# A Fourier and retention trunk on one core: homes for the start slots, an earlier split of h, gates ahead of rstd

## The chip, the core and the metric

The kernel runs on one core of a Trainium2 chip. The metric is the time of one execution on the device in microseconds (us). The engines are named as in the profile: PE (TensorE; PEld is its weight load), DVE (VectorE), ACT (ScalarE), POOL (GpSimd), SP (SyncE, which here only issues DMAs).

## The reference

Two layers work on 512 latent and 256 context tokens of width 1024. Each layer norms its input and modulates it by rows that come from the condition vectors `c` and `c_ctx` (`ada_params`). Layer 0 mixes by a grouped 2-D Fourier transform, layer 1 by bidirectional retention with four heads. Both gate with `silu(z)` and project back.

```
def ada_params(cond, w, b):
    m = jax.nn.silu(cond) @ w + b
    return jnp.split(m, 3, axis=-1)
def fourier_mixer(h, w_in, w_out):
    u, z = jnp.split(h @ w_in, 2, axis=-1)
    y = jnp.fft.fft2(ug, axes=(1, 3), norm='ortho').real     # ug: u in 8 groups of 256
    return (y * jax.nn.silu(z)) @ w_out
def ret_output(o, z, w_out):
    o = o * lax.rsqrt(jnp.mean(o * o, axis=-1, keepdims=True) + EPS)
    return (o * jax.nn.silu(z)) @ w_out
    ...
    hl = rmsnorm(x, norm_g[i]) * (1.0 + sc_l[:, None, :]) + sh_l[:, None, :]
    x = x + gt_l[:, None, :] * ol
```

## The kernel before, in words

**Weights.** All weights come in one stream of 512 KB slots, `stream[t]`, issued by SP in order. A slot lands in one of three buffers of `raw`, is split by ACT into a rounded part (`hi`) and by DVE into the rest (`lo`), both into `ring`, and PE multiplies with three matmuls per product (`mm3`). SP waits before each load until the buffer's last user is done.

**Start.** Slots 0 to 15 hold the adaptive norm's weights of layer 0 and aren't split. The string `START` says who consumes slot t: `P` is PE (`ada_tile`, 16 matmul records on the raw tile), `D` is DVE (`early`, two dot products with the condition rows `cond_rows`). Slots 0 to 7, all for PE, give the scale; all eight must be done before DVE can make the factor `fmul`. Beside them the six token tiles `x_tok` arrive. ACT squares them (`x_root`), DVE inverts the roots (`x_rstd`), folds tile pairs (`x_fold`) and splits them with ACT (`x_hi`, `x_lo`). Then PE runs the token transform `transform(k)` for k = 0 to 7, with an `ada_tile` of slots 9, 11, 13 and 15 behind k = 0 to 3. After each transform ACT and DVE write its two parts (`transform_lo`), and DVE runs `early` of slots 8, 10, 12 and 14 between them. Slots 8 to 15 give the shift (`add_shift`), which the second half of U group 0 needs. A load of slot t waits for the user of slot t - 3.

**U groups.** `project_u(g)` for eight groups, then `features`. Meanwhile POOL makes h (`tmp_t`). After group 7, ACT and DVE split the slots z0 and z1, the U result (`u_hi`, `u_lo`), and copy and combine the features (`copy_q`, `sum_diff`); then they split h in eight parts (L791, L1258). PE's next work, `gates(0, 0)`, waits for all of group 7's split (`u_lo_done`) and for part k of h at its step k. It writes the context halves to bank 2, which group 7 has used.

**Last head.** After the last head, PE starts the output projection `out_pair(SLOT_OUT1, ...)`. At step 3 it sums the squares (`o_sum`, L1856). ACT takes the root, DVE the reciprocal (L1390). DVE then multiplies the four head outputs with it into `p_f` (L1408), and `p_f` is multiplied into the gates, two of them by POOL (L643) and two by DVE (L1412). Only then does DVE split slot 2 of the output weights (L1038), which PE needs for step 8. The queue order on each engine is that of the code.

Of the kernel before, what the change touches and what calls it, by code (L numbers as in the profile page):

```python
# [66 lines left out]
START = "PPPPPPPPDPDPDPDP"  # L67
DVE_SHIFT = 4
# [13 lines left out]
    "u": (SLOT_U, 3, 1, (6, 5, 5)),  # L82
    "z": (SLOT_Z, 3, 2, (11, 11, 10)),
    "out0": (SLOT_OUT0, 2, 0, (27, 27, 26)),
    "head": (SLOT_HEAD, 3, 2, (35, 35, 26)),
    "out1": (SLOT_OUT1, 2, 0, (51, 51, 42)),
# [71 lines left out]
def build(nc, x_lat, x_ctx, x_rows, small_in, cond_in, decay_in, stream, tables_in, middle_in,  # L158
          middle_w_in, rope_in, out):
    ctx = ExitStack()  # L160
    with ctx:
# [72 lines left out]
        squares = gate[:, 11 * D:12 * D].bitcast(mybir.dt.bfloat16).rearrange("p (b n) -> p b n", b=2)  # L234
# [44 lines left out]
        fold = xreg[:, 4128:4128 + 2 * SLOT].rearrange("p (b n) -> p b n", b=2)  # L279
        q_f = gate[:, TT * D + P + 2 * TOK:TT * D + P + 2 * TOK + NF]  # L280
# [43 lines left out]
        s_raw = [sem(f"raw_in{i}") for i in range(RAW_BUFS)]  # L324
        s_xt, s_rope, s_out = sem("x_columns_in"), sem("rope_in"), sem("out_stored")
# [58 lines left out]
        def _(sp):  # L384
# [16 lines left out]
            def load_start(t):  # L401

                if t >= RAW_BUFS:
                    used(t - RAW_BUFS)
                buf = raw_at("start", t)[0]
                sp.dma_start(raw[:, buf, :], stream[t]).then_inc(s_raw[buf], 16)

            def load_x(t):
                sp.dma_start(x_tok[:, t, :], x_rows[t]).then_inc(s_x[t], 16)

            load_x(0)
            load_x(1)
            load_start(0)
            load_x(2)
            load_x(3)
            load_start(1)
            load_x(4)
            load_x(5)
            load_start(2)
# [40 lines left out]
        def _(pool):  # L460
# [178 lines left out]
            def gate_head(h, tiles=range(4)):  # L639
                for i in tiles:  # L640
# [22 lines left out]
            gate_head(HEADS - 1, (0, 2))  # L663
# [10 lines left out]
        def _(act):  # L674
# [22 lines left out]
            def x_root(t):  # L697
                act.wait_ge(s_x[t], 16)
                if t >= 2:
                    act.wait_ge(tok_sq, t - 1)  # L700
# [322 lines left out]
        def _(dve):  # L1023
# [165 lines left out]
            for k in range(KT):  # L1189
                transform_lo(k)  # L1190
                if k < DVE_SHIFT - 1:
                    early(KT + 2 * k + 2)
# [921 lines left out]
```

## Time and profile before

| | us |
|---|---|
| median of 3 runs | 985.59 (983.39 to 987.88) |
| the profiled execution | 989.9 |
| its span, first to last instruction | 988.1 |
| PE busy / DVE busy / ACT busy / POOL busy in it | 941.5 / 547.6 / 345.0 / 258.7 |

Times inside the execution are counted from the start of the span. The mean granted clock of PE was 0.977 of full speed; a stretch at 0.50 is at the lower of its two levels (1.2 of 2.4 GHz).

### The profile page before, as it was taken

What the parts mean: (1) busy time and instruction counts of PE and PEld (TensorE: products, weight loads), DVE (VectorE), ACT (ScalarE), POOL (GpSimd) and SP (SyncE); (2) the same over time, 40 slices, a digit from 0 to 9 for tenths busy, and PEclk for the clock granted to TensorE, in tenths of its full rate; (3) what the DMA queues carried; (4) which work ended last, traced back from release to release, by engine and by line L of the source; (5) the groups of instructions that cost most, each with busy time, mean ns of one, the idle gap of its engine ahead of it and who ended that gap; (6) DMA issues with size and microseconds to landing.
All of it is one profiled execution on the core that took longest, in us unless ns stands there. A gap on an engine that the chain in (4) does not pass through costs nothing.

```text
span 988.1 us, 13089 instructions
## 1 busy us (share of the span) xinstructions
PE 941.5 (95%) x4838; PEld 811.9 (82%) x4838; DVE 547.6 (55%) x810; ACT 345.0 (35%) x582; POOL 258.7 (26%) x251
## 2 busy tenths in 40 slices
PE   5899998999999999959999999999999999998996
PEld 5798998888888888847888888887888888876886
DVE  4666876999985332358344355426434445456433
ACT  6342434333314332334333333324223333453222
POOL 3338970477764000014100131014100321011001
PEclk9899999999999999979999999999999999998998
DMA  7645332565555211211222021102211121102222
GB/s 300 221 157 181 121 110 86 180 193 183 192 172 229 68 64 64 85 42 48 81 64 65 22 86 64 65 22 69 80 64 42 42 69 58 64 1 81 90 86 86
DMA packets 28858, 98.70 MB, mean 100 GB/s; under 512 B 3816, under 2 KB 6024, under 8 KB 28560
## 3 DMA queue, kind: packets, MB, share of 16 engines
q1 hardware_dynamic: 26384, 89.86, 27.1%
q0 software_dynamic: 2032, 7.89, 2.2%
q8 instruction: 26, 0.43, 0.2%
q10 hardware_dynamic: 400, 0.39, 0.1%
q14 instruction: 16, 0.13, 0.0%
HBM read 96.01 MB, written 2.10 MB: 99 GB/s over the span
## 4 chain that ended last, share of the span: by engine, by line
PE 85%; DVE 6%; DMA 3%; POOL 2%; issue 2%; ACT 1%; SPq 0%; POOLq 0%; DVEq 0%; ACTq 0%
PE banks L1618 27%; PE banks L1619 27%; PE banks L1620 27%; DMA raw<-stream 3%; PE banks L1671 2%; DVE hreg L1373 1%; POOL gate L643 1%; DVE xreg L1432 1%; DVE gate L1367 1%; DVE ring L1038 1%; DVE gate L1397 0%; POOL gate L636 0%; POOL xreg L653 0%; PE banks L1856 0%; POOL gate L670 0%
## 5 line engine op out<-in xcount | busy, mean ns | idle before, releaser
L1618 PE MATMUL banks<-hreg,ring 128*128 128x512 f32 (+2 forms) x940 | 336.4, 358 | 19.9 <-DVE hreg L1373 9.1
L1619 PE MATMUL banks<-hreg,ring 128*128 128x512 f32 (+2 forms) x940 | 333.8, 355 | 0.0
L1620 PE MATMUL banks<-hreg,ring 128*128 128x512 f32 (+2 forms) x940 | 331.3, 352 | 0.0
L1038 DVE TENSOR_TENSOR ring<-raw,ring 128x512 fp32r<-128x512 f32 x192 | 134.8, 717 | 272.9 <-ACT ring L682 272.2
L682 ACT ACTIVATE ring<-raw 128x512 fp32r<-128x512 f32 x192 | 119.5, 630 | 387.7 <-PE banks L1620 313.2
L1618 PEld LDWEIGHTS banks<-hreg,ring 128*128 128x128 f32 x940 | 178.8, 190 | 48.3 <-issue 12.9
L1620 PEld LDWEIGHTS banks<-hreg,ring 128*128 128x128 f32 x940 | 178.4, 190 | 22.9
L1619 PEld LDWEIGHTS banks<-hreg,ring 128*128 128x128 f32 x940 | 178.9, 190 | 22.0 <-issue 1.0
L603 POOL TENSOR_TENSOR gate<-xreg,gate 128x257 f32<-128x257 f32 (+1 forms) x64 | 81.5, 1304 | 68.6 <-ACT gate L817 51.3
L1070 DVE CUSTOM_DVE_ANT_0 dist<-raw,gate 128x1024 bf16<-128x1024 f32 x64 | 90.5, 1414 | 3.8
L636 POOL TENSOR_TENSOR gate<-gate 128x512 f32<-128x512 f32 x12 | 16.8, 1397 | 250.7 <-ACT gate L891 249.9
L1618 PE MATMUL banks<-ring,hreg 128*128 128x512 f32 x192 | 74.7, 389 | 0.0
L1619 PE MATMUL banks<-ring,hreg 128*128 128x512 f32 x192 | 74.7, 389 | 0.0
L1620 PE MATMUL banks<-ring,hreg 128*128 128x512 f32 x192 | 74.7, 389 | 0.0
L1618 PE MATMUL banks<-wreg 128*128 128x512 f32 (+2 forms) x192 | 71.8, 374 | 0.0
L1619 PE MATMUL banks<-wreg 128*128 128x512 f32 (+2 forms) x192 | 71.2, 371 | 0.0
L1620 PE MATMUL banks<-wreg 128*128 128x512 f32 (+2 forms) x192 | 71.1, 370 | 0.0
L1619 PE MATMUL banks<-wreg,ring 128*128 128x512 f32 (+2 forms) x172 | 58.8, 342 | 0.0
L1620 PE MATMUL banks<-wreg,ring 128*128 128x512 f32 (+2 forms) x172 | 58.4, 339 | 0.0
L1618 PE MATMUL banks<-wreg,ring 128*128 128x512 f32 (+2 forms) x172 | 58.3, 339 | 0.0
L1671 PE MATMUL banks<-csf,raw 128*128 128x128 f32 x192 | 30.4, 328 | 16.6 <-DMA raw<-stream 16.6
L651 POOL TENSOR_TENSOR xreg<-xreg 128x512 f32<-128x512 f32 x8 | 10.4, 1295 | 126.1 <-DVE xreg L1432 126.1
(214 smaller groups left out, 1142.2 us busy)
## 6 DMA issues: line engine op xcount, KB each, us to landing
raw<-stream SPq DMA_DIRECT2D x160, 512.0 KB, 3.3
gate<-x_rows SPq DMA_DIRECT2D x6, 512.0 KB, 6.8
gate<-x_lat POOLq DMA_DIRECT2D x1, 2048.0 KB, 8.8
xreg<-x_lat POOLq DMA_DIRECT2D x1, 2048.0 KB, 9.2
gate<-cond_in POOLq DMA_DIRECT2D x2, 512.0 KB, 7.2
gate<-x_ctx POOLq DMA_DIRECT2D x1, 1024.0 KB, 11.5
xreg<-x_ctx POOLq DMA_DIRECT2D x1, 1024.0 KB, 12.0
xreg<-tables_in SPq DMA_DIRECT2D x1, 775.0 KB, 11.5
```

Of the source, the lines that this page charges most:

```text
L603: pool.tensor_tensor(g, y, g, ALU.mult).then_inc(gated, 1)
L636: pool.tensor_tensor(head_rstd, head_rstd, p_f[:, i % 2, :], ALU.add).then_inc(oacc, 1)
L643: pool.tensor_tensor(g, g, p_f[:, i % 2, :], ALU.mult).then_inc(ogated, 1)
L651: pool.tensor_tensor(turn[0], turn[0], turn[1], ALU.subtract).then_inc(summed, 1)
L682: act.activation(ring[:, n % 2, 0, c], raw[:, buf, c], ACT.Copy).then_inc(hi_done, 1)
L1038: dve.tensor_tensor(ring[:, n % 2, 1, c], raw[:, buf, c], f32(ring[:, n % 2, 0, c]), ALU.subtract).then_inc(split_done, 1)
L1070: dve.tensor_tensor_reduce(out=dot_out, in0=raw[:, buf, :], in1=cond_rows[:, v, :], scale=1.0, scalar=0.0, op0=ALU.mult, op1=ALU.add, accu ...
L1367: dve.tensor_tensor(tmp_t[:, k, 0:LAT], tmp_t[:, k, 0:LAT], rstd_t[:, 0:LAT], ALU.mult).then_inc(t_vec, 1)
L1618: pe.matmul(out, left[0], right[0], start=start, stop=False)
L1619: pe.matmul(out, left[0], right[1], start=False, stop=False)
L1620: return pe.matmul(out, left[1], right[0], start=False, stop=stop)
L1671: last = pe.matmul(o, raw[:, buf, P * k:P * k + P], csf[:, k:2 * KT:KT].unsqueeze(1).to_broadcast([P, WARM, 2]), start=k == 0, stop=k == K ...
```

## The change

It has three independent parts.

1. **Start.** Slots 3 to 8 get places of their own (`ada_home`: the two `fold` buffers, a free piece of `gate`, and token tiles 0, 2 and 1 once those are used up), so that with the three `raw` buffers nine slots have one each. The condition rows are loaded by SP behind slot 5, no longer by POOL. The small decay load goes behind slot 8. Slot 15 is consumed by DVE in place of PE (`START` ends in `DD`, `DVE_SHIFT` is 5). ACT loads the root table ahead of the first token tile, and squares token tile 5 before it waits for the reciprocal of tile 4, which DVE makes earlier. The first `add_shift` and `fold_lo(0)` both stand after transform 5.
2. **End of the U groups.** ACT and DVE split parts 0 and 1 of h ahead of the second half of z1 and of group 7's result, part 2 ahead of `copy_q(6)` and `sum_diff(6)`. PE no longer waits for group 7's split before `gates(0, 0)`, whose context halves go to bank 7.
3. **Last head.** DVE multiplies the four outputs into their gates before the reciprocal (`last_products`). Behind the reciprocal DVE splits slot 2 first, then DVE and POOL multiply two gates each with the reciprocal in place.

```
-START = "PPPPPPPPDPDPDPDP"
-DVE_SHIFT = 4
+START = "PPPPPPPPDPDPDPDD"
+DVE_SHIFT = 5
...
+        ada_home = [fold[:, 0, :], fold[:, 1, :], gate[:, 11 * D:12 * D], x_tok[:, 0, :],
+                    x_tok[:, 2, :], x_tok[:, 1, :]]
+        def ada_slot(t):
+            if RAW_BUFS <= t <= KT:
+                return ada_home[t - RAW_BUFS], s_ada[t - RAW_BUFS], 16
+            buf, landed = raw_at("start", t if t < RAW_BUFS else t - len(ada_home))
+            return raw[:, buf, :], s_raw[buf], landed
...
             def load_start(t):
-                if t >= RAW_BUFS:
-                    used(t - RAW_BUFS)
+                if t in (6, 7):
+                    sp.wait_ge(pair_done, 2 * (t - 5))
+                if t == KT:
+                    sp.wait_ge(xs_lo, 2)
+                if t > KT:
+                    used(t - RAW_BUFS if t > KT + RAW_BUFS else t - KT - 1)
...
+            for t in range(3, 6):
+                load_start(t)
+            for v in range(2):
+                sp.dma_start(cond_rows[:, v, :], cond_in[v].partition_broadcast(P)).then_inc(s_cond, 16)
+            for t in (6, 9, 7, 10, 8):
+                load_start(t)
             sp.dma_start(dk[:, 0, :], decay_in.partition_broadcast(P)).then_inc(s_decay, 16)
-            for t in range(RAW_BUFS, SLOT_U):
+            for t in range(11, SLOT_U):
                 load_start(t)
...
-            pool.wait_ge(s_x[TT - 1], 16)
-            for v in range(2):
-                pool.dma_start(cond_rows[:, v, :], cond_in[v].partition_broadcast(P)).then_inc(s_cond, 16)
...
-            gate_head(HEADS - 1, (0, 2))
+            pool.wait_ge(orstd, HEADS)
+            for i in (0, 2):
+                pool.wait_ge(onorm, 4 * (HEADS - 1) + i + 1)
+                g = gate1[:, FT - 4 + i, :]
+                pool.tensor_tensor(g, g, head_rstd, ALU.mult).then_inc(ogated, 1)
...
             act.activation(csf[:, :], small[:, 0:16], ACT.Silu).then_inc(csf_done, 1)
+            act.activation(small[:, 0:1], eps[:, :], ACT.Sqrt).then_inc(warm, 1)
...
             x_root(4)
+            x_root(5)
             act.wait_ge(tok_rstd_done, 5)
...
-            x_root(5)
...
-            u_hi(GROUPS - 1)
-            copy_q(GROUPS - 2)
             act.wait_ge(slot_done, 2 * SLOT_Z + DONE0)
             for k in range(KT):
                 act.wait_ge(h_made, 2 * k + 2)
                 act.activation(h_hi[:, k, :], tmp_t[:, k, :], ACT.Copy).then_inc(hhi_done, 1)
+                if k == 1:
+                    hi("z", 1, SLOT_Z + 1, halves=(1,))
+                    u_hi(GROUPS - 1)
+                if k == 2:
+                    copy_q(GROUPS - 2)
...
+            def last_products():
+                dve.wait_ge(z1_done, 4 * HEADS)
+                for i in range(4):
+                    dve.wait_ge(osq, 4 * (HEADS - 1) + i + 1)
+                    g = gate1[:, FT - 4 + i, :]
+                    dve.tensor_tensor(g, bank(2 + i), g, ALU.mult).then_inc(onorm, 1)
...
+            last_products()
             for kk in range(8, 12):
                 g1_lo(kk)
             o_rstd(HEADS - 1)
+            lo("out1", 2, RING_OUT1 + 2)
             last_norm()
-            lo("out1", 2, RING_OUT1 + 2)
...
-                lat, ctx_out = (3 * q, 3 * q + 1), 3 * q + 2
+                lat, ctx_out = (3 * q, 3 * q + 1), 7 if first else 3 * q + 2
...
-            pe.wait_ge(u_lo_done, 2 * GROUPS)
             gates(0, 0, first=True)
```

SP's queue at the start, before (a load of a start slot reads `raw<-stream`; behind the third one, the tables, the decay row, then slots 3 to 15):

```order
L406 DMA raw<-stream 128x1024
L420 DMA xreg<-tables_in 128x1550
L422 DMA dk<-decay_in 128x8
L406 DMA raw<-stream 128x1024 [waits ada_slot_used] x8
L406 DMA raw<-stream 128x1024 [waits early_dot_done]
L406 DMA raw<-stream 128x1024 [waits ada_slot_used]
```

And of the change (slots 3, 4 and 5, the condition rows, then slots 6, 9, 7, 10, 8, the decay row, 11 and 12, 13):

```order
L429 DMA xreg<-tables_in 128x1550
L420 DMA xreg<-stream 128x1024 x2
L420 DMA gate<-stream 128x1024
L434 DMA gate<-cond_in 128x1024 x2
L420 DMA gate<-stream 128x1024 [waits x_folded]
L420 DMA raw<-stream 128x1024 [waits ada_slot_used]
L420 DMA gate<-stream 128x1024 [waits x_folded]
L420 DMA raw<-stream 128x1024 [waits ada_slot_used]
L420 DMA gate<-stream 128x1024 [waits x_lo_done]
L437 DMA dk<-decay_in 128x8
L420 DMA raw<-stream 128x1024 [waits ada_slot_used] x2
L420 DMA raw<-stream 128x1024 [waits early_dot_done]
```

Five transfers between the tables and slot 6 no longer wait for anything, and the waits of slots 6, 7 and 8 are on the folding and splitting of the tokens and no longer on PE's tiles.

DVE at the end of the U groups, before (`ring` are the halves of z0 and z1, `wreg` is group 7's split, `xreg` is `sum_diff(6)`, `hreg` the parts of h):

```order
L1038 TENSOR_TENSOR ring<-raw,ring 128x512 x4
L1215 TENSOR_TENSOR wreg<-banks,wreg 128x386 x2
L1225 TENSOR_TENSOR xreg<-banks,gate 128x386 x2
L1258 TENSOR_TENSOR hreg<-gate,hreg 128x768 x8
```

And of the change:

```order
L1056 TENSOR_TENSOR ring<-raw,ring 128x512 x3
L1274 TENSOR_TENSOR hreg<-gate,hreg 128x768 x2
L1056 TENSOR_TENSOR ring<-raw,ring 128x512
L1234 TENSOR_TENSOR wreg<-banks,wreg 128x386 x2
L1274 TENSOR_TENSOR hreg<-gate,hreg 128x768
L1244 TENSOR_TENSOR xreg<-banks,gate 128x386 x2
L1274 TENSOR_TENSOR hreg<-gate,hreg 128x768 x5
```

Two parts of h now stand ahead of five other instructions; nothing is added.

DVE behind the last head, before (`hreg` are the splits of gates 6 to 11, then the reciprocal, norms and gates, slots 2 and 3, the splits of gates 12 to 15):

```order
L1417 TENSOR_TENSOR hreg<-gate,hreg 128x512 x6
L1390 RECIPROCAL gate<-gate 128x512
L1408 TENSOR_TENSOR gate<-banks,gate 128x512 x2
L1412 TENSOR_TENSOR gate<-gate 128x512
L1408 TENSOR_TENSOR gate<-banks,gate 128x512 x2
L1412 TENSOR_TENSOR gate<-gate 128x512
L1038 TENSOR_TENSOR ring<-raw,ring 128x512 x4
```

And of the change:

```order
L1427 TENSOR_TENSOR gate<-banks,gate 128x512 x4
L1439 TENSOR_TENSOR hreg<-gate,hreg 128x512 x4
L1411 RECIPROCAL gate<-gate 128x512
L1056 TENSOR_TENSOR ring<-raw,ring 128x512 x2
L1435 TENSOR_TENSOR gate<-gate 128x512 x2
L1056 TENSOR_TENSOR ring<-raw,ring 128x512 x2
L1439 TENSOR_TENSOR wreg<-gate,wreg 128x512 x4
```

Nothing stands between the reciprocal and the split of slot 2 any more; the four multiplications that stood there are ahead of the reciprocal.

## Rows read from the trace of the kernel before

**Rows 1.** The page, part 4: the chain that ended last, by engine.

```profile
PE 85%; DVE 6%; DMA 3%; POOL 2%; issue 2%; ACT 1%; SPq 0%; POOLq 0%; DVEq 0%; ACTq 0%
```

**Rows 2.** Windows, an undisturbed stretch: A:B length, busy, clock, DMA share, GB/s.

```profile
75.00:155.00 80.00, 80.00 (x451) 77.22 (x450) 55.00 (x85) 29.22 (x55) 63.47 (x57) 1.00 0.37 129
```

**Rows 3.** The page, part 6: issues, KB each, median us to landing.

```profile
raw<-stream SPq DMA_DIRECT2D x160, 512.0 KB, 3.3
...
gate<-cond_in POOLq DMA_DIRECT2D x2, 512.0 KB, 7.2
```

**Rows 4.** The chain in order of time, start: start us, us, what.

```profile
19.84 5.48 PE banks L1671 x32
...
25.34 7.25 DMA raw<-stream
...
32.63 3.79 PE banks L1671 x16
...
44.50 5.76 DMA raw<-stream
...
56.44 1.83 PE banks L1671 x16
...
60.80 0.17 PE banks L1618
```

**Rows 5.** Timelines of PE, POOL, ACT, DVE, start: start us, us, instruction [idle before].

```profile
7.87 6.89 PE L1671 MATMUL banks<-csf,raw 128*128 128x128 f32 x32 [7.87 <-DMA raw<-stream]
15.26 2.06 PE L1671 MATMUL banks<-csf,raw 128*128 128x128 f32 x16 [0.49 <-DMA raw<-stream]
...
39.51 2.00 PE L1671 MATMUL banks<-csf,raw 128*128 128x128 f32 x16
...
50.31 2.64 PE L1671 MATMUL banks<-csf,raw 128*128 128x128 f32 x16 [1.92 <-DMA raw<-stream]
...
17.24 2.85 POOL L523 CAST wreg<-xreg 128x516 fp32r<-128x516 f32 x2 [14.71 <-DMA xreg<-tables_in]
...
6.42 1.28 ACT L704 ACT_TABLE_LOAD   x1
...
19.51 1.15 ACT L723 ACTIVATE gate<-gate,dist 128x1024 f32<-128x1024 f32 x1 [3.10 <-DVE dist L1105]
...
29.21 1.22 DVE L1127 TENSOR_TENSOR ring<-gate,ring 128x1024 fp32r<-128x1024 f32 x1
...
65.64 1.28 DVE L1056 TENSOR_TENSOR ring<-xreg,ring 128x512 fp32r<-128x512 f32 x2
```

**Rows 6.** Windows, while the condition rows are in flight.

```profile
26.00:28.00 2.00, 2.00 (x20) 2.00 (x20) 2.00 (x2) 1.98 (x2) 0.00 (x0) 1.00 0.82 152
```

**Rows 7.** Timelines of ACT, DVE and PE at the U groups' end.

```profile
153.44 0.63 ACT L682 ACTIVATE ring<-raw 128x512 fp32r<-128x512 f32 x1 [1.44 <-PE banks L1620]
...
155.59 5.98 ACT L791 ACTIVATE hreg<-gate 128x768 fp32r<-128x768 f32 x8
...
156.67 7.03 DVE L1258 TENSOR_TENSOR hreg<-gate,hreg 128x768 fp32r<-128x768 f32 x8
...
157.76 0.77 PE L1618 MATMUL banks<-hreg,ring 128*128 128x512 f32 x1 [2.60 <-DVE hreg L1258]
```

**Rows 8.** Windows, PE behind three of its waits (the clock stands before the DMA share).

```profile
157.76:162.00 4.24, 4.24 (x15) 3.62 (x16) 4.24 (x6) 3.81 (x6) 0.00 (x0) 0.64 0.02 4
896.67:902.00 5.33, 5.33 (x14) 4.19 (x15) 4.17 (x7) 0.02 (x1) 0.00 (x0) 0.54 0.61 185
50.31:56.44 6.13, 6.13 (x40) 6.13 (x41) 2.88 (x6) 0.00 (x0) 0.14 (x1) 0.72 0.70 215
```

**Rows 9.** The chain behind the last head.

```profile
887.55 3.36 DVE gate L1390
...
896.02 0.61 DVE ring L1038
```

**Rows 10.** Timeline of PE behind the last head.

```profile
896.67 0.80 PE L1618 MATMUL banks<-hreg,ring 128*128 128x512 f32 x1 [4.42 <-DVE ring L1038]
```

More of the change, by code:

```diff
@@ L81 @@
     "start": (0, 3, 0, (0, 0, 0)),
[L82 to L86, printed above, removed]
+    "u": (SLOT_U, 3, 1, (4, 3, 3)),
+    "z": (SLOT_Z, 3, 2, (9, 9, 8)),
+    "out0": (SLOT_OUT0, 2, 0, (25, 25, 24)),
+    "head": (SLOT_HEAD, 3, 2, (33, 33, 24)),
+    "out1": (SLOT_OUT1, 2, 0, (49, 49, 40)),
 }
@@ L324, in build @@
         s_raw = [sem(f"raw_in{i}") for i in range(RAW_BUFS)]
+        s_ada = [sem(f"ada_in{i}") for i in range(RAW_BUFS, KT + 1)]
         s_xt, s_rope, s_out = sem("x_columns_in"), sem("rope_in"), sem("out_stored")
@@ L637, in norm_head, with gate_head @@
                                        ALU.add).then_inc(oacc, 1)
-            def gate_head(h, tiles=range(4)):
-                for i in tiles:
+            def gate_head(h):
+                for i in range(4):
                     pool.wait_ge(onorm, 4 * h + i + 1)
@@ L674, in _, with hi @@
         def _(act):
-            def hi(phase, n, r, i=0, per=0):
+            def hi(phase, n, r, i=0, per=0, halves=(0, 1)):
                 buf, landed = raw_at(phase, n)
                 act.wait_ge(s_raw[buf], raw_step(phase, per) * i + landed if per else landed)
-                for a in range(2):
+                for a in halves:
                     c = slice(a * SLOT // 2, (a + 1) * SLOT // 2)
@@ L698, in x_root @@
                 act.wait_ge(s_x[t], 16)
-                if t >= 2:
-                    act.wait_ge(tok_sq, t - 1)
-                act.activation(squares[:, t % 2, :], x_tok[:, t, :], ACT.Square,
+                act.activation(squares, x_tok[:, t, :], ACT.Square,
                                accum_out=tok_ss[:, t:t + 1]).then_inc(tok_sq, 1)
@@ L814, in gates @@
                     for a, b, src in ((0, LAT, bank(3 * q + half)),
-                                      (LAT, TOK, bank(3 * q + 2, CTX, CTX * half))):
+                                      (LAT, TOK, bank(7 if first else 3 * q + 2, CTX, CTX * half))):
                         kk = 2 * j + half if split is not None else gate0_at(2 * j + half)
@@ L1030, in link, with lo @@
                 dve.wait_ge(step, steps[0])
-            def lo(phase, n, r):
+            def lo(phase, n, r, halves=(0, 1)):
                 buf = raw_at(phase, n)[0]
-                for a in range(2):
+                for a in halves:
                     c = slice(a * SLOT // 2, (a + 1) * SLOT // 2)
@@ L1130, in early @@
             def early(t):
-                buf, landed = raw_at("start", t)
+                src, s_landed, landed = ada_slot(t)
                 d = START[:t].count("D")
-                dve.wait_ge(s_raw[buf], landed)
+                dve.wait_ge(s_landed, landed)
                 dve.wait_ge(cond_rows_done, 2)
@@ L1191, in _ @@
                 if k < DVE_SHIFT - 1:
-                    early(KT + 2 * k + 2)
-                if k == 4:
+                    early((10, 12, 14, 15)[k])
+                if k == 5:
                     dve.wait_ge(early_dot, 2 * DVE_SHIFT)
@@ L1259, in _ @@
                                   ALU.subtract).then_inc(hlo_done, 1)
+                if k == 1:
+                    lo("z", 1, SLOT_Z + 1, halves=(1,))
+                    u_lo(GROUPS - 1)
+                if k == 2:
+                    sum_diff(GROUPS - 2)
             def gates(jj, q, split=None, first=False, last=False):
@@ L1666, in ada_tile @@
             def ada_tile(t, o):
-                buf, landed = raw_at("start", t)
-                pe.wait_ge(s_raw[buf], landed)
+                src, s_landed, landed = ada_slot(t)
+                pe.wait_ge(s_landed, landed)
                 for k in range(KT):
-                    last = pe.matmul(o, raw[:, buf, P * k:P * k + P],
+                    last = pe.matmul(o, src[:, P * k:P * k + P],
                                      csf[:, k:2 * KT:KT].unsqueeze(1).to_broadcast([P, WARM, 2]),
```

59 lines of the change are left out of this document (24 added, 35 removed).

## The prediction

> **What bounds the kernel now.** I read the page first, then the chain in order of time, then the timelines and windows around the chain's steps that aren't PE. PE carries 85% of the chain [rows 1], and between 75 and 155 us it is busy for all of 80.00 us at clock 1.00 [rows 2]: there nothing is to be won without taking work from PE. The reader should look for the places where PE stands still, and for the clock behind them. There are three groups.
>
> At the start the chain goes from load to tile and back: tiles 3 and 4, the load of slot 7 that was issued at 25.34 once tile 4 had given its buffer back and took 7.25 us, tile 7 from 32.63 to 36.42, and later the load of slot 13, 5.76 us from 44.50 [rows 4], for which PE stood still for 1.92 us [rows 5]. At the end of the U groups PE waits 2.60 us for the first part of h [rows 7]. Behind the last head it waits 4.42 us [rows 10] for slot 2, which DVE splits only after the reciprocal, the norms and the gates [rows 9].
>
> Each wait is paid twice. Behind them PE ran at a mean clock of 0.64 for 4.24 us, 0.54 for 5.33 us, and 0.72 for 6.13 us [rows 8], with the lower level in them. What a stretch lost is its length times what its clock lacks of 1: 1.53, 2.45 and 1.72 us.
>
> **Part 1, the start.** The question is when slot 7 lands. From slot 0 (tile 0 starts at 7.87) to slot 2 (15.26) six 512 KB transfers landed [rows 5], so one took 7.39 / 6 = 1.23 us, or 426 GB/s, with the queue full. The tables landed at 17.24 [rows 5]. But slot 3, which is behind the decay row, let tile 3 start only at 19.84 [rows 4], 2.6 us later in place of 1.23. In the change the decay row is behind slot 8, and slots 3, 4, 5, two condition rows, 6, 9 and 7 follow the tables, none with a wait that isn't over by then (the last one, on the fold of tiles 2 and 3, is over before the second split of tokens starts). Eight transfers by 1.23 put slot 7 at 27.1. The condition rows may cost more: while they were in flight, 152 GB/s moved at a busy share of 0.82 [rows 6], 185 GB/s for full engines. At that rate their 1.05 MB take 5.7 us and not 2.5, and slot 7 lands at 30.3. Those are the two bounds; slot 7's other traffic speaks for neither, and I take the middle, 28.7.
>
> PE has tiles 3 to 7 to run from 18.5. At full clock one takes 1.83 us, and tiles 3 and 4, partly at the lower level, took 5.48 together [rows 4]; 18.5 + 5.48 + 3 x 1.83 = 29.5 even so. So the load still decides: tile 7 ends at 28.7 + 1.83 = 30.5, against 36.42: **5.9 us**. Tokens are no bound: their last split ended at 30.43 [rows 5], is wanted only by the last operands of the first transform, and the change takes up to 1.28 (the table load ahead of the first tile) and 3.10 us (ACT's wait for a reciprocal) [rows 5] out of that chain. These two edits I cost at nothing more; without them the tokens would end about when they are wanted.
>
> The first transform then runs without half clock: it took 39.51 - 36.42 = 3.1 us [rows 4, 5], a later one 60.80 - 58.27 = 2.5 [rows 4]: **0.6 us**. Slot 15's tile leaves PE: **1.8 us** [rows 4]. DVE takes its two dots, and with them the first shift and the fold's split (1.28 us [rows 5]) move together behind transform 5. I estimate that `transform_lo(6)` is 1 us late and PE starts U group 0 that much later. This costs next to nothing, since its second half waits for the shift of parts 4 to 7 anyhow; should the pile reach that shift, it costs at most the 1.28.
>
> What becomes of the wait for slot 13? Its load is let go by DVE's dots of slot 10, behind the first `transform_lo`, and the transforms run to where it is wanted at the same distance as before. Slots 12 and 14 are in flight beside it as before, so I take the same 5.76 us, and the 1.92 + 1.72 = 3.6 us stay. The page's median is 3.3 us [rows 3]; with that, slot 13 would be there in time. The Trainium skill, "DMA: Bandwidth & Descriptors", section "Anatomy of one DMA", gives a fixed 2.0 us and the bytes at 436 GB/s, 3.2 us for 512 KB by my estimate; the median agrees, this load does not. By that rule the sum for the start would be 3.6 us larger.
>
> Start: 5.9 + 0.6 + 1.8 = 8.3 us. Bounds: slot 7 at 30.3 and tile 7 at half clock (3.79 us [rows 4]) end at 34.1, 3.6 later, and the 0.6 goes too: 4.1. Tile 7 at 29.5 and slot 13 in time: 8.3 + 1.0 + 3.6 = 12.9.
>
> **Part 2, the U groups' end.** ACT is let go by PE's last U matmul at 153.44; one part of h costs it 5.98 / 8 = 0.75, and DVE 7.03 / 8 = 0.88 us [rows 7]. So part 0 is split at 155.1, and PE is free at 157.76 - 2.60 = 155.2. The wait goes, with the loss of clock behind it: 2.60 + 1.53 = **4.1 us**. What is late next is group 7's split, the second half of z1 and `sum_diff(6)`. PE wants them at its step 4 and behind it, and one step ahead of them (six matmuls on 512 and six on 256 columns) costs it more than the 0.88 of a part of h. Parts 1 to 3 keep ahead. Bank 7 costs nothing, as its last reader was group 0. The lower bound is 2.3, a few tenths of wait and the clock lost all the same.
>
> **Part 3, the last head.** The reciprocal ends at 887.55 + 3.36 = 890.91 [rows 9]. The first half of slot 2 then costs 0.61 [rows 9] and is there at 891.5; PE reaches step 8 at 896.67 - 4.42 = 892.25 [rows 10]. The wait goes and so does the loss behind it: 4.42 + 2.45 = **6.8 us**. The four products come ahead, while POOL still adds squares and DVE waits, so the reciprocal needn't be later. It has 0.7 us to give. Behind slot 2 the gates now take one pass each, on two engines, and the second slot and gates 12 to 15 are wanted four steps later. The lower bound is 4.0.
>
> Sum: 8.3 + 4.1 + 6.8 = 19.2 us. The profiled execution took 989.9, and would take 970.7. It is 4.3 above the median of the runs, 985.59; against that I predict 985.59 - 19.2 = **966.4 us**.
>
> **Rivals.**
> - *Slot 13 lands in time.* The shorter queue gives it 3.3 us, as most loads have [rows 3]; against it stands that its neighbours in flight are the same. 22.8 us gained: 962.8. The page's rule named above says this too. 0.18.
> - *The condition rows are slow.* They go ahead of slots 6, 9 and 7 in one queue, where before they had POOL's own. Windows during their flight speak for it [rows 6], the 7.2 us to landing of two of them beside other loads [rows 3] against more. Tile 7 ends at 34.1; 15.0 gained: 970.6. 0.12.
> - *The tiles become the bound.* If PE runs tiles 3 to 7 at the lower level throughout, they take 5 x 3.79 = 19.0 from 18.5 and end at 37.4. The start then gives tile 15 alone, 12.7 in all: 972.9. Tiles 3 and 4 together at 5.48 speak against it [rows 4]. 0.05.
> - *Short waits stay at both ends.* Margins there are 0.1 and 0.7 us. If about 1 us comes back and the clock falls as before, the 1.53 + 2.45 return: 14.2 gained, 971.4. 0.07.
> - *Slower than before.* The condition rows are 128 copies of one source row. If these copies were served one engine at a time, at 426 / 16 = 27 GB/s, both would take 39 us in front of slot 7, 37 more than I count, and the kernel would take 1003. It turns slower than before by 0.5% where the two rows take 24 us more than I count, 19.2 + 4.9. The 7.2 us in [rows 3] speak against it. 0.03.
>
> The Trainium skill, same page, section "Queues, rings and completion order", says that an engine goes round between queue rows packet by packet and keeps ring order in one row. By that the two condition rows stand wholly ahead of slot 7, as in my count of eight transfers, which rests on the order of issue and the 1.23 us alone.
>
> **How the numbers follow.** My forecast has 0.55. Its own range is 964 to 969. The low end of the range is the first rival with tile 7 at its early bound, 961.8, less 1.3 for the spread of the runs; the high end takes in the cases up to 972.9 and 2 for that spread: 960.5 to 975. About 0.5% (4.9 us) is what a measurement tells from no change. All cases but the last are faster by more than that. I leave 0.04 for no difference, for things that add up and that I don't see, and 0.03 for slower: faster 0.93.
>
> **What would show it.** Tile 7 ends near 30.5 (between 29 and 34), the first transform lasts 2.5 us, the wait for slot 13 is still about 1.9 with the clock down behind it, transforms end 8 us earlier. PE goes from features to `gates(0, 0)` with no more than 0.3 us between, and the clock stays at 1.00; the same ahead of step 8 behind the last head, where slot 2's first half ends near 0.7 us before PE wants it. I am wrong if the token chain or the condition rows hold the first transform, if the clock falls where PE has no wait, or if a gain comes back as a wait of the gates' dots on DVE.

## The result, and the profile after

The changed kernel takes 970.4 us (median; 970.2 to 970.58, 4 runs) against 985.79 (983.39 to 987.88, 4 runs) of the kernel before: the ratio is 0.9849, 95% interval 0.9825 to 0.9874, a gain of 15.4 us. The prediction was 966.4 with a range of 960.5 to 975. The measured time lies inside that range and outside the forecast's own 964 to 969. The profiled executions stand further apart, 989.9 and 970.25: 19.65 us.

The page of the changed kernel, parts 1 (cut), 4 and 6. PE's share of the chain is as in [rows 1]; the six homes appear as loads of their own, and the condition rows now take 15.1 us to land, because they wait in a full queue ([rows 3]: 7.2 on GpSimd's queue).

```profile
span 968.4 us, 13062 instructions
...
PE 85%; DVE 7%; DMA 2%; POOL 2%; issue 2%; ACT 1%; POOLq 0%; SPq 0%; DVEq 0%; ACTq 0%
...
gate<-stream SPq DMA_DIRECT2D x4, 512.0 KB, 13.3
...
gate<-cond_in SPq DMA_DIRECT2D x2, 512.0 KB, 15.1
```

The chain of the changed kernel in order of time, start; it answers to [rows 4].

```profile
15.55 13.06 DMA gate<-stream
...
28.66 2.05 PE banks L1694 x16
...
38.07 5.12 DMA raw<-stream
43.24 2.05 PE banks L1694 x16
...
50.15 1.91 DVE dist L1156
52.11 2.18 DVE dist L1156
...
57.83 1.20 DVE ring L1074 x2
59.10 1.07 DVE hreg L1188 x2
60.21 0.45 PE banks L1641
...
73.25 0.86 PE banks L1795 x2
```

Slot 7 landed at 28.6 and tile 7 ended at 30.71. Slot 13's load is still on the chain. New is the last part: VectorE's work stands ahead of the first U projection. The timelines of PE, VectorE and GpSimd show it (with the idle time before an instruction in brackets); they answer to [rows 5].

```profile
43.24 2.05 PE L1694 MATMUL banks<-csf,raw 128*128 128x128 f32 x16 [1.29 <-DMA raw<-stream]
...
60.21 0.45 PE L1641 MATMUL banks<-hreg,ring 128*128 128x386 f32 x1 [1.95 <-DVE hreg L1188]
...
45.56 1.23 DVE L1156 CUSTOM_DVE_ANT_0 dist<-raw,gate 128x1024 bf16<-128x1024 f32 x1
...
50.07 1.99 DVE L1156 CUSTOM_DVE_ANT_0 dist<-raw,gate 128x1024 bf16<-128x1024 f32 x1
...
52.11 2.18 DVE L1156 CUSTOM_DVE_ANT_0 dist<-raw,gate 128x1024 bf16<-128x1024 f32 x1
...
49.70 1.29 POOL L561 TENSOR_TENSOR xreg<-raw 128x512 f32<-128x512 f32 x1
50.94 2.26 POOL L555 TENSOR_TENSOR xreg<-raw 128x512 f32<-128x512 f32 x1
53.16 2.28 POOL L561 TENSOR_TENSOR xreg<-raw 128x512 f32<-128x512 f32 x1
```

Slot 14's dot takes 1.23 us. Slot 15's two take 1.99 and 2.18 while GpSimd folds beside them, and GpSimd's two folds take 2.26 and 2.28 instead of 1.29. After 52.11 every VectorE instruction up to the split of transform 6 is late, and PE waits 1.95 us. VectorE itself had stood still before slot 15's dots, for a transform that ran behind slot 13's tile:

```profile
48.94 0.16 DVE L1186 COPY dc<-banks 128x2 f32<-128x2 f32 x1 [2.14 <-ACT hreg L754]
```

At the U groups' end and behind the last head the waits of [rows 7] and [rows 10] are gone. This is PE's timeline at the U groups' end; behind the last head PE's timeline has no wait between 874 and 905.

```profile
146.43 0.47 PE L1641 MATMUL banks<-hreg,ring 128*128 128x512 f32 x1 [0.26 <-DVE hreg L1274]
```

The windows that answer to [rows 8], behind slot 13, at the U groups' end and behind the last head; the clock stands before the DMA share, and it is 1.00 in all three.

```profile
42.00:50.00 8.00, 6.76 (x59) 6.76 (x59) 5.08 (x12) 2.10 (x4) 5.82 (x13) 1.00 0.79 272
145.00:150.00 5.00, 4.74 (x27) 4.02 (x26) 4.67 (x8) 5.00 (x10) 0.00 (x0) 1.00 0.22 63
884.00:890.00 6.00, 6.00 (x28) 4.92 (x27) 4.25 (x7) 1.78 (x3) 0.00 (x0) 1.00 0.47 151
```

**A ruler for all that follows.** The two matmuls of `ones` on `diag` between U groups 0 and 1 stand in every chain as "0.86 PE banks ... x2". I call their start the mark. Up to it a kernel has its start and U group 0; behind it come the other U groups, the layers and the last head. Before, the mark is at 82.24 us; changed, at 73.25: 8.99 less. The matmuls of `ones` on `acc_t` at the end of layer 0 (1.14 us, x2) moved from 432.54 to 419.82, 12.72 less; part 2 is the only edit between the two places, so the U groups' end gave 3.73. The whole gained 19.7 in the span, so the rest, the last head, gave 7.0.

### The profile page after: what moved, and what is told of

It reads as the page before. It is cut to its first block, busy times and chain, and to the rows that moved or that the text cites. A ratio compares the mean times of both kernels' runs of the same rounds, so it can differ in the third digit from the quotient of the medians.

```text
span 968.4 us, 13062 instructions
## 1 busy us (share of the span) xinstructions
PE 929.1 (96%) x4822; PEld 800.6 (83%) x4822; DVE 557.7 (58%) x814; ACT 344.2 (36%) x583; POOL 258.9 (27%) x249
## 4 chain that ended last, share of the span: by engine, by line
PE 85%; DVE 7%; DMA 2%; POOL 2%; issue 2%; ACT 1%; POOLq 0%; SPq 0%; DVEq 0%; ACTq 0%
PE banks L1641 28%; PE banks L1642 28%; PE banks L1643 28%; DMA gate<-stream 1%; DVE hreg L1394 1%; POOL gate L655 1%; DVE xreg L1454 1%; DVE dist L1156 1%; DVE gate L1388 1%; DMA raw<-stream 1%; DVE ring L1056 1%; DVE hreg L1188 1%; DVE gate L1418 0%; POOL gate L648 0%; DMA gate<-x_rows 0%
## 5 line engine op out<-in xcount | busy, mean ns | idle before, releaser
L1056 DVE TENSOR_TENSOR ring<-raw,ring 128x512 fp32r<-128x512 f32 x192 | 143.0, 761 | 264.1 <-ACT ring L698 263.3
L615 POOL TENSOR_TENSOR gate<-xreg,gate 128x257 f32<-128x257 f32 (+1 forms) x64 | 73.2, 1174 | 73.2 <-ACT gate L835 56.7
L1088 DVE CUSTOM_DVE_ANT_0 dist<-raw,gate 128x1024 bf16<-128x1024 f32 x64 | 84.8, 1325 | 3.8
L1641 PE MATMUL banks<-wreg 128*128 128x512 f32 (+2 forms) x192 | 71.0, 370 | 0.0
L1642 PE MATMUL banks<-wreg 128*128 128x512 f32 (+2 forms) x192 | 70.5, 367 | 0.0
L1643 PE MATMUL banks<-wreg 128*128 128x512 f32 (+2 forms) x192 | 70.4, 367 | 0.0
L1641 PEld LDWEIGHTS banks<-ring,hreg 128*128 128x128 f32 x192 | 36.0, 188 | 7.5
## 6 DMA issues: line engine op xcount, KB each, us to landing
gate<-cond_in SPq DMA_DIRECT2D x2, 512.0 KB, 15.1
```

The lines of the kernel that those rows point to most:

```text
L615: pool.tensor_tensor(g, y, g, ALU.mult).then_inc(gated, 1)
L1056: dve.tensor_tensor(ring[:, n % 2, 1, c], raw[:, buf, c], f32(ring[:, n % 2, 0, c]), ALU.subtract).then_inc(split_done, 1)
L1088: dve.tensor_tensor_reduce(out=dot_out, in0=raw[:, buf, :], in1=cond_rows[:, v, :], scale=1.0, scalar=0.0, op0=ALU.mult, op1=ALU.add, accu ...
L1641: pe.matmul(out, left[0], right[0], start=start, stop=False)
L1642: pe.matmul(out, left[0], right[1], start=False, stop=False)
L1643: return pe.matmul(out, left[1], right[0], start=False, stop=stop)
```

## The experiments

### Which part gave what, and why the profiled executions differ by more than the medians

Three kernels each have one part of the change, and a fourth is the kernel before again. Part 1 alone has all of the diff that concerns homes, loads, `START`, ScalarE's order and the first shift; its edit against the kernel before begins so:

```diff
-START = "PPPPPPPPDPDPDPDP"
-DVE_SHIFT = 4
+START = "PPPPPPPPDPDPDPDD"
+DVE_SHIFT = 5
```

> The start of the change alone; the U groups' end and the last head are as before. In the profiles the start gave 9.0 us of 19.7, but the medians differ by 15.4 only, since the profiled run of before was 4.1 us above its median. Theory A (the 4.1 us are scatter of the start: when the loads land): against the median of before this is worth 9.0 - 4.3 = about 4.7 us, ratio 0.995. Theory B (they are scatter of the clock behind the two late waits): this is worth 9.0 us, ratio 0.991.

Part 2 alone, the split of h:

```diff
-            u_hi(GROUPS - 1)
-            copy_q(GROUPS - 2)
...
+                if k == 1:
+                    hi("z", 1, SLOT_Z + 1, halves=(1,))
+                    u_hi(GROUPS - 1)
```

> The split of h ahead of the last U group alone. The profiles show 3.7 us at this place (2.3 of wait, 1.5 of half clock, with 0.26 of wait left). Theory A: 3.7 us against the median, ratio 0.9962. Theory B: the half clock is not paid in the median run, and 2.3 us are left, ratio 0.9977.

Part 3 alone, the last head:

```diff
+            last_products()
             for kk in range(8, 12):
                 g1_lo(kk)
             o_rstd(HEADS - 1)
+            lo("out1", 2, RING_OUT1 + 2)
             last_norm()
-            lo("out1", 2, RING_OUT1 + 2)
```

> The gates of the last head ahead of rstd alone. The profiles show 7.0 us (4.4 of wait, 2.45 of half clock). Theory A: 7.0 us, ratio 0.9929. Theory B: the half clock is not paid in the median run: 4.4 us, ratio 0.9955. A third theory, that the parts help each other, would show as a sum of the three that is well under the 15.4 us of the whole.

The kernel before, with no edit:

> The kernel before once more, for a second profile and as a measure of the comparison: ratio 1.000 within 0.2%. Theory A: where its span differs from 988.1 us, the difference lies ahead of the row-sum matmuls of U group 1 (82.24 us in the first profile), and from there to the end it takes 905.9 us again. Theory B: the difference lies behind the waits of the U groups' end and the last head, in the granted clock there.

| kernel | median us (runs) | ratio to before, 95% | span, profiled | mark | mark to end |
|---|---|---|---|---|---|
| before, first profile | 985.79 (4) | | 988.1 | 82.24 | 905.9 |
| before again | 985.54 (12) | 1.0006 [0.9983, 1.0028] | 985.0 | 78.98 | 906.0 |
| part 1 alone | 980.3 (10) | 0.994 [0.992, 0.9959] | 979.1 | 73.19 | 905.9 |
| part 2 alone | 981.8 (12) | 0.9961 [0.9939, 0.9983] | 981.6 | 79.38 | 902.2 |
| part 3 alone | 977.54 (9) | 0.9924 [0.9899, 0.9948] | 975.7 | 77.44 | 898.3 |
| changed | 970.4 (4) | 0.9849 [0.9825, 0.9874] | 968.4 | 73.25 | 895.2 |

The kernel before ran beside them at 985.52 (980.75 to 990.04, 30 runs), so the parts gave 5.2, 3.7 and 8.0 us by medians, 16.9 together against 15.4 measured at once; with intervals of about 2 us on each, that is agreement. Part 2's interval alone (0.9939 to 0.9983) takes in theory B's 0.9977 too; the last two columns say more. In the profiled executions the time from the mark to the end is the same wherever the start ended: 905.9, 906.0 and 905.9 with neither part 2 nor 3. Part 2 takes 3.7 off it and part 3 7.6. The mark itself, with the old start, was found at 82.24, 78.98, 79.38 and 77.44. In these executions the scatter lies in the start, and the execution on which I built the sum was the latest of the four. Theory A holds for them. (With all three parts, the time from the mark to the end was 894.7 to 895.8 in nine kernels, so about 1 us of scatter lies behind the mark as well.)

What differs is seen in the kernel before again. PE's timeline, tile 7, slot 13's tile and slot 15's:

```profile
31.73 3.58 PE L1671 MATMUL banks<-csf,raw 128*128 128x128 f32 x16 [2.69 <-DMA raw<-stream]
...
46.68 2.00 PE L1671 MATMUL banks<-csf,raw 128*128 128x128 f32 x16
...
52.98 2.06 PE L1671 MATMUL banks<-csf,raw 128*128 128x128 f32 x16 [1.78 <-DMA raw<-stream]
```

Two windows of the same kernel, with these tiles in them:

```profile
30.00:40.00 10.00, 8.27 (x59) 8.27 (x60) 4.52 (x14) 3.06 (x4) 7.54 (x28) 0.83 0.51 193
50.00:60.00 10.00, 8.22 (x72) 8.07 (x71) 4.06 (x11) 2.11 (x4) 5.00 (x4) 1.00 0.55 184
```

Slot 7 landed 0.9 us earlier than in the first profile [rows 4]. Slot 13 was in time, where the first profile had PE wait 1.92 us for it; here PE waited for slot 15 instead, 1.78 us, with no slow clock behind it: 1.00 where [rows 8] show 0.72. With part 2 alone PE waited 0.60 us for slot 13, with part 3 alone not at all, both at full clock. The 1.92 us of wait and the 1.72 us of lost clock that I took for a part of the kernel were a part of one execution.

### The new wait: slot 13, or VectorE's queue

Part 1 alone, which has the same start, had slot 13 in time, and still the mark came at 73.19, as in the changed kernel where slot 13 was waited for. So either VectorE's queue ends beside slot 13's wait, or something gives the gain back. Four kernels test it. First, slot 15's dots earlier in VectorE's order:

```diff
-                if k < DVE_SHIFT - 1:
-                    early((10, 12, 14, 15)[k])
+                for t in {0: (10,), 1: (12,), 2: (14, 15)}.get(k, ()):
+                    early(t)
```

> The changed kernel with one edit: VectorE forms slot 15's two dots right behind slot 14's, ahead of its part of transform 3, instead of behind it. Theory Q (what bounds the new start is VectorE's queue behind transform 5, made long because slot 15's dots run at 2.0 and 2.2 us beside GpSimd's folding instead of 1.22): the dots lie at 46.8 to 49.3, cost 1.2 each, TensorE starts the first U projection without the wait of 1.95 us, and the median is 1.9 below the changed kernel's 970.4: 968.5 (968.0 to 969.0). The rival, theory S (the wait of 1.95 is only where the lateness of slot 13 shows, as the prediction had it, and the queue costs next to nothing by itself): another wait takes its place in front of the first U projection, and the time stays within 0.5 of 970.4.

Second, the load of slot 13 no longer behind slot 10's dots:

```diff
+            if t in (12, 13):
+                return ada_home[t - 12], s_ada[t - 12], 32
...
-                    used(t - RAW_BUFS if t > KT + RAW_BUFS else t - KT - 1)
+                    used(t - 5 if t > 13 else t - KT - 1)
```

(The buffers of slots 14 and 15 and of the slots behind them shift along.)

> The changed kernel with slots 12 and 13 loaded into the two folding buffers (free after tiles 3 and 4) instead of the raw buffers, so that slot 13 no longer waits for slot 10's dots; slots 14 and 15 then take the raw buffers of slots 9 and 10. Theory Q: slot 13's wait of 1.29 us goes, the eight transforms end about 57.0 instead of 58.3, and the wait in front of the first U projection grows from 1.95 to about 3.2, so that the time stays where it is: 970.4 (969.9 to 970.9). Theory S (slot 13's landing is the bound): 1.3 less, 969.1 (968.6 to 969.6).

Third, both, and the first shift a transform earlier:

```diff
-                if k == 5:
+                if k == 4:
                     dve.wait_ge(early_dot, 2 * DVE_SHIFT)
...
                     add_shift(0, KT // 2)
-                    fold_lo(0)
+                if k == 5:
+                    fold_lo(0)
```

> The changed kernel with both edits (slots 12 and 13 in the folding buffers, slot 15's dots ahead of transform 3 on VectorE) and a third: the bias and the first half of the shift stand behind transform 4 instead of transform 5 on VectorE. Theory Q: with the queue short, slot 13's 1.3 us now shows too: 1.95 + 1.3 = 3.2 less than 970.4, 967.2 (966.5 to 968.2). Theory S: 1.3 less, 969.1, as with the buffers alone. If neither holds and another engine or landing takes the place, the time lies between 968.2 and 970.4 and the trace names it in front of the first U projection.

Fourth, slot 15 back on PE:

```diff
-START = "PPPPPPPPDPDPDPDD"
-DVE_SHIFT = 5
+START = "PPPPPPPPDPDPDPDP"
+DVE_SHIFT = 4
```

> The changed kernel with slot 15 given back to TensorE (tile behind transform 3, as before the change), so that VectorE forms the dots of four slots instead of five. It measures the term of 1.8 us that the prediction gave for slot 15's tile leaving TensorE. The prediction's sum: 1.8 more, 972.2 (971.7 to 972.7). Theory Q: TensorE ends the transforms 1.8 later, but VectorE's queue is 4.2 us shorter (dots of 2.0 and 2.2), so that the wait of 1.95 in front of the first U projection goes: 970.3 (969.8 to 970.8), and the move of slot 15 was worth nothing by itself.

| kernel | median us (lowest to highest) | ratio to before, 95% | span | first transform starts | U group 0 starts | wait ahead of it | mark |
|---|---|---|---|---|---|---|---|
| changed | 970.4 (970.2 to 970.58) | 0.9849 [0.9825, 0.9874] | 968.4 | 30.47 | 60.21 | 1.95 | 73.25 |
| part 1 alone | 980.3 (979.41 to 982.11) | 0.994 [0.992, 0.9959] | 979.1 | 30.23 | 58.66 | 2.29 | 73.19 |
| dots earlier | 968.82 (967.59 to 970.87) | 0.9821 [0.9796, 0.9846] | 969.0 | 30.55 | 58.67 | 1.92 | 73.22 |
| slot 13 early | 970.12 (968.67 to 971.24) | 0.9834 [0.9808, 0.9859] | 968.2 | 30.18 | 58.79 | 1.94 | 73.34 |
| both, shift earlier | 969.89 (968.57 to 970.71) | 0.9834 [0.9809, 0.986] | 966.9 | 30.53 | 58.63 | 1.96 | 71.59 |
| slot 15 on PE | 970.28 (968.85 to 972.42) | 0.9837 [0.981, 0.9864] | 968.9 | 30.20 | 60.74 | 0.87 | 73.70 |

*Slot 13 early.* The median, 970.12, is the one that theory Q gave, but not for Q's reason. Q had VectorE's queue hold the first U projection in place, with a wait of 3.2. The wait stayed at 1.94 and U group 0 started 1.4 earlier, as theory S had it. VectorE had been held by slot 13 too: its idle time ahead of slot 15's dots fell from 2.14 to 0.70.

```profile
47.16 0.16 DVE L1192 COPY dc<-banks 128x2 f32<-128x2 f32 x1 [0.70 <-ACT hreg L760]
```

So PE and VectorE don't end side by side by chance; VectorE's end hangs on the transforms, and these on slot 13. From the first transform to U group 0 it took 29.74 us in the changed kernel, which is 28.45 and slot 13's wait of 1.29; part 1 alone, with slot 13 in time, took 28.43. What was won went into the clock: U group 0's first 3.7 us ran at 0.67, and from its start to the mark it took 14.55 us where 13.04 is the changed kernel's. The same loss is in part 1 alone (14.53):

```profile
58.66 0.45 PE L1631 MATMUL banks<-hreg,ring 128*128 128x386 f32 x1 [2.29 <-DVE hreg L1182]
```

*Slot 15 on PE.* The tile's move was worth little: the mark came 0.45 later where the prediction's term asked for 1.8, and the median was 970.28 where it asked for 972.2. PE's wait ahead of U group 0 fell by 1.08 in exchange.

*Dots earlier.* The median was 1.6 lower, near Q's 968.5, but with runs up to 970.87 and the mark unmoved. The wait did not go, which is against Q. Slot 13 was in time in that execution, so the kernel to compare with is part 1 alone, and from the first transform to U group 0 the earlier dots saved 0.3 us. The chain of that kernel:

```profile
58.67 0.57 PE banks L1641
59.24 0.32 PE banks L1642
...
73.22 0.86 PE banks L1795 x2
```

Its VectorE timeline:

```profile
47.68 1.22 DVE L1156 CUSTOM_DVE_ANT_0 dist<-raw,gate 128x1024 bf16<-128x1024 f32 x1 [0.72 <-DMA raw<-stream]
...
48.94 1.22 DVE L1156 CUSTOM_DVE_ANT_0 dist<-raw,gate 128x1024 bf16<-128x1024 f32 x1
...
53.87 1.21 DVE L1107 TENSOR_TENSOR mod<-row_mod,small 128x10 f32<-128x10 f32 x1
```

The dots are back at 1.22, but the bias beside GpSimd's folding now takes 1.21 (0.15 in the changed kernel). U group 0 starts at 58.67 and not 60.21, and its matmuls then take 0.32 instead of 0.18 us: the lower clock level, up to 62.1. The mark is where it was, and the 1.5 us are spent on the clock. With both edits the same wait, 1.96 us, had no slow clock behind it, and the mark came at 71.59. Theory Q's 3.2 us did not come (1.7 by the mark, 0.5 by the median); VectorE lost 1.9 us here, in its timeline:

```profile
52.26 1.02 DVE L1204 TENSOR_TENSOR dist<-dc,fmul 128x8 f32<-128x8 f32 x1
53.31 1.40 DVE L1206 SCALAR_TENSOR_TENSOR dist<-mod,dist 128x4 f32<-128x4 f32 x2
```

They take 0.17 and 0.36 where GpSimd doesn't fold; here its folds ran from 49.5 to 54.5.

### Three details of the start, and a better version

The shift back behind transform 5, with both edits kept:

> The changed kernel with slots 12 and 13 in the folding buffers and slot 15's dots ahead of transform 3, the bias and the shift left behind transform 5. With the shift behind transform 4 its small operations lay beside GpSimd's folding and took 1.02 and 1.21 us where 0.17 and 0.36 is usual, about 2 us together. Theory P (VectorE and GpSimd hinder each other; what counts is which of VectorE's work lies beside the folding): the small operations come after the folding, VectorE ends its part of transform 6 at 57.5 instead of 58.5, the wait in front of the first U projection falls from 1.96 to 0.9, and the time is 1.1 less than with the shift behind transform 4: 968.8 (968.0 to 969.5). Theory C (what is left of the loss is TensorE's clock, which falls behind the wait in most executions and gives about 1.7 us back): with the wait under 1 us the clock holds and the gain is 1.1 + 1.7: 967.1 (966.5 to 967.8). If the place of the shift doesn't matter: 969.9.

The decay row ahead again:

```diff
+            sp.dma_start(dk[:, 0, :], decay_in.partition_broadcast(P)).then_inc(s_decay, 16)
             for t in range(3, 6):
                 load_start(t)
...
-            sp.dma_start(dk[:, 0, :], decay_in.partition_broadcast(P)).then_inc(s_decay, 16)
```

> The changed kernel with one edit: the decay row's load goes back ahead of slot 3 in SyncE's queue. It measures the part of the start's gain that the prediction put on the row's stall of the queue. By the prediction: tile 7 ends 1.4 later (32.1 instead of 30.7) and, with transforms and slot 13 moving along, the time is 1.4 more: 971.8 (971.3 to 972.3). The rival: the row's descriptors stall nothing when the queue is full behind them: 970.4 (969.9 to 970.9).

The condition rows on GpSimd's queue again:

```diff
+            pool.wait_ge(s_x[TT - 1], 16)
+            for v in range(2):
+                pool.dma_start(cond_rows[:, v, :], cond_in[v].partition_broadcast(P)).then_inc(s_cond, 16)
             pool.wait_ge(xs_lo, 6)
...
-            for v in range(2):
-                sp.dma_start(cond_rows[:, v, :], cond_in[v].partition_broadcast(P)).then_inc(s_cond, 16)
```

> The changed kernel with one edit: the two condition rows are loaded again by GpSimd's queue, once the last token tile has landed, instead of by SyncE's behind slot 5. The prediction took the bytes as served at the same 420 GB/s wherever they stand. By it: the rows share the engines with slots 3 to 7 instead of standing ahead of slots 6 to 8, tile 7 ends within 0.5 of 30.7, and the time is 970.4 (969.9 to 971.0). The rival (two queues at once, the second with small descriptors, make each other slower): slots 3 to 7 land 1 to 3 us later, tile 7 ends at 32 to 34, and the time is 972 to 973.5.

The condition rows in SyncE's queue, but behind slot 7, with both edits:

```diff
-            for t in (6, 9, 7, 10, 8):
+            for t in (6, 9, 7):
+                load_start(t)
+            for v in range(2):
+                sp.dma_start(cond_rows[:, v, :], cond_in[v].partition_broadcast(P)).then_inc(s_cond, 16)
+            for t in (10, 8):
                 load_start(t)
```

> The changed kernel with slots 12 and 13 in the folding buffers, slot 15's dots ahead of transform 3, and the two condition rows behind slot 7 in SyncE's queue instead of ahead of slot 6. With the rows on GpSimd's queue, tile 7 ended at about 27.6 instead of 30.7, but the rows landed at 32.9 and everything behind them was late. Theory R (the 1 MB of rows holds slots 6 and 7 back by 2.5 us, and they can land at about 28.7 without harm): the first transform starts at 27.6, slot 8's dots at 30.8 instead of 31.8, TensorE waits for VectorE once at the end of the transforms, and the first U projection starts at about 57.5 instead of 59.1: 1.6 less than the 969.5 with the rows ahead, 967.9 (967.0 to 969.0). The rival, theory V (VectorE's queue is the bound from the first dots on, whatever TensorE gains): the wait in front of the first U projection grows to 3 us or more, TensorE's clock falls behind it, and the time is 969.5 to 970.5.

| kernel | median us (lowest to highest) | ratio to before, 95% | span | first transform starts | U group 0 starts | wait ahead of it | mark |
|---|---|---|---|---|---|---|---|
| shift behind 5 | 969.47 (967.46 to 970.61) | 0.9835 [0.9811, 0.9858] | 967.1 | 31.96 | 59.08 | 0.71 | 72.07 |
| decay row ahead | 972.23 (971.17 to 973.02) | 0.9866 [0.9844, 0.9888] | 969.4 | 31.77 | 60.19 | 2.27 | 74.67 |
| rows on GpSimd's queue | 973.89 (972.89 to 975.53) | 0.9885 [0.9864, 0.9906] | 971.3 | 27.44 | 63.58 | 1.94 | 76.54 |
| rows behind slot 7 | 967.9 (965.79 to 969.85) | 0.9824 [0.9797, 0.985] | 965.4 | 27.25 | 55.99 | 2.61 | 70.54 |

*Shift behind 5.* The small operations were short again, the wait was 0.71 and the clock held, as theories P and C both had it. But the median, 969.47, lies at the top of P's range and misses C's. In the profiled execution slot 6 landed late (15.23 us after its issue), PE ran tiles 6 and 7 behind that wait at a mean clock of 0.70, and the first transform started 1.5 later than in the changed kernel; from there to the mark it took 40.1 us against 42.8. So the profile shows a shorter path behind the first transform, and the median does not confirm that the whole kernel keeps it. With five runs from 967.5 to 970.6 a difference of 1 us isn't settled.

*Decay row.* The first transform starts 1.3 later, the median is 1.8 more. That is the expected 1.4 within the scatter. Slot 13 was in time in this execution, so the nearer comparison is part 1 alone: the first transform, U group 0 and the mark are each 1.5 later.

*Rows on GpSimd's queue.* Both theories missed. The rows neither shared the engines with slots 3 to 7 nor slowed them: GpSimd issued them only at 26.9, behind its work on the tables, and they landed at 32.85. PE had its tiles early (27.44), then slot 8's dots, slot 10's and slot 13's load were late, and PE stood for 5.78 us with the lower clock behind. The chain:

```profile
21.23 4.97 POOL wreg L541 x2
26.90 5.95 DMA gate<-cond_in
...
41.20 3.47 DMA raw<-stream
```

PE's timeline, slot 13's tile:

```profile
44.71 3.77 PE L1695 MATMUL banks<-csf,raw 128*128 128x128 f32 x16 [5.78 <-DMA raw<-stream]
```

The wait of 1.94 ahead of U group 0 had full clock behind it here. To have the rows issued by SyncE is worth 3.5 us of part 1's gain by the medians, 3.3 by the mark.

*Rows behind slot 7.* Theory R gave 967.9, and 967.9 was measured. The path was another: R had U group 0 at 57.5, it started at 55.99, and the lower clock behind it took 1.5 us back. That the two agree is in part luck. All six runs lie below the lowest of the changed kernel's four. The two kernels were timed beside different runs of the kernel before and their intervals overlap, so "faster than the changed kernel" rests on those runs and on the mark, 2.7 earlier. It holds for the three edits together; the place of the rows alone is the 1.6 us to "shift behind 5", whose runs overlap with these. The first transform starts 3.2 earlier; at its end VectorE is the bound (wait 2.61), and some clock is lost behind it. PE's timeline:

```profile
55.99 0.44 PE L1649 MATMUL banks<-hreg,ring 128*128 128x386 f32 x1 [2.61 <-DVE hreg L1196]
```

The chain: a shift operation of 0.17 us that takes 1.01 beside GpSimd, a U matmul at the lower clock level, and the mark.

```profile
51.80 1.01 DVE dist L1206
...
57.67 0.32 PE banks L1651
...
70.54 0.86 PE banks L1803 x2
```

## Why the prediction was right, point by point

**The start, predicted 8.3.** Against the profile that it was worked from, 8.99. Three of its pieces stood: slot 7 landed at 28.6 (28.7 taken), tile 7 ended at 30.71 (30.5 taken), and the first transform ran at full clock. The bound of slow condition rows did not occur: about 420 GB/s moved while they were in the queue. Three pieces failed, and that their errors nearly cancel is luck:
- "I take the same 5.76 us, and the 1.92 + 1.72 = 3.6 us stay": slot 13 took 5.12 us, the wait was 1.29, and no clock was lost, 2.3 us better than taken. By the 3.2 us that the prediction estimated from the Trainium skill ("DMA: Bandwidth & Descriptors", section "Anatomy of one DMA") it was further off than by the row; the skill gives the two figures behind it for loads that GpSimd issues, and SyncE issued this one.
- "Slot 15's tile leaves PE: 1.8 us": with the tile back on PE the time was 970.28 and the mark 0.45 later. The term was worth a quarter of what it was put at, because PE waits for VectorE in its place; it and the next piece are two sides of one exchange.
- "This costs next to nothing": `transform_lo(6)` was late enough for PE to wait 1.95 us. The sum left out that GpSimd's folds and VectorE's dots make each other slower, 1.7 us over slot 15's two dots. Given back are the 1.95 less the 0.68 that PE waited for the second half before, 1.3 of the 1.8 us.

**The U groups' end, predicted 4.1.** 3.7 by the profiles and by the part alone; a wait of 0.26 stays, as the prediction allowed.

**The last head, predicted 6.8.** 7.0 in the changed kernel, 7.6 by the mark in the part alone; the 0.6 between them is not explained. PE has no wait there and the clock stays at 1.00.

**The sum, 19.2, and where it was taken off.** The profiled executions gave 19.65. The step that failed is "It is 4.3 above the median of the runs, 985.59; against that I predict 985.59 - 19.2". Taken off the execution it was read from, the same sum gives 970.7, and 970.4 was measured. The 4.3 us were waits and lost clock of the start, which the change removes once: the mark of the first profile was 2.9 to 4.8 later than in three more executions of the old start. That the median execution did not have them is an estimate, as it was not profiled: each of the four marks less what its own execution lay above its kernel's median (4.3, 1.3, 1.7 and 0) gives 77.4 to 77.9, about 4.5 us ahead of the first profile's mark. The 966.4 thus takes them off a time that does not hold them. What is left, 0.3, is inside the scatter of the runs.

**The rivals.** Slot 13 in time (962.8) came true in some executions of the new start (part 1 alone, dots earlier, decay row ahead). U group 0 then started 1.3 to 1.6 us sooner behind the first transform, and the lower clock behind it took 1.5 us back, so that it was worth nothing. The tiles, slow rows and waits that stay at both ends did not occur; that the rival of slow rows had 970.6, nearly the measured time, is chance. Nothing spoke for slower.

## What to carry to other kernels

Take a sum off the execution from which its waits were read, and ask which of these waits another execution of the same kernel would show. Where a part is removed from the engine that waits, look at the engine that it goes to up to the next point where the first one waits for it: here PE gave up a tile of 1.8 us and waited 1.3 us more for VectorE. And look at the clock behind that point: three times U group 0 started 1.4 to 1.6 us earlier (part 1 alone, dots earlier, slot 13 early), and the mark did not move, because the lower clock level took it back. What goes ahead in a full queue costs its bytes to everyone behind it, so place a load by when it is wanted, and on an engine that is free to issue it.

## What the runs showed of the hardware

- VectorE's dot of 128 x 1024 took 1.22 us alone and 1.99 to 2.35 beside a GpSimd fold; the fold took 1.29 alone and up to 2.29. Small VectorE operations of 0.17 us took 1.02 there. Behind the last head the two halves of slot 2's split took 2.32 us together beside GpSimd's gates, where one alone took 0.61 before. VectorE's transform splits, which read PSUM, stayed at 1.14 beside the same folds. The Trainium skill, "SBUF — State Buffer", section "SBUF: two separate sides", says that VectorE with two SBUF inputs and GpSimd take turns on a shared port pair for whole instructions; the numbers agree with that, and no run here tests it by itself.
- A wait of 1.9 to 2.0 us ahead of the U projections was followed by the lower clock in two executions (dots earlier, slot 13 early) and by full clock in three (changed; both, shift earlier; rows on GpSimd's queue); waits of 2.27, 2.29 and 2.61 by the lower one, waits of 0.71 and 0.87 by full clock. From U group 0's start to the mark it took 14.48 to 14.55 us with the lower clock and 12.96 to 13.04 without, so it cost 1.5 us each time. With the old start, too: a wait of 1.92 for slot 13 with it, one of 1.78 for slot 15 without. What decides it stays open.
- The small decay row (4 KB in 128 copies) ahead of slot 3 delayed the first transform by 1.3 us against the changed kernel and by 1.5 against part 1 alone, a little more than a 512 KB load takes in the full queue (1.23).
- The old start scattered by 5.3 to 9.2 us in sets of 9 to 12 runs (9.3 us over 30). Kernels with the new one scattered by 0.4 to 4.1 us over 4 to 10 runs each.
